# A two-block transformer kernel: masks in row tiles, a weight split on VectorE, and the last cross-attention head in halves

## The reference, cut to what matters

```python
# forgetting heads, per block of 128 queries
logits = einsum('bhqd,bhkd->bhqk', q_b, k) * scale
logits = logits + F_b[..., :, None] - F[..., None, :]
logits = where(k_pos[None, :] <= q_pos[:, None], logits, NEG_INF)
p = softmax(logits);  out = einsum('bhqk,bhkd->bhqd', p, v)
# differential heads: mask is k // 64 <= q // 64
p = softmax(masked l1) - lam * softmax(masked l2)
# cross-attention, 4 heads of 256, after both layers' mixers
q = split_heads(rms_norm(x) @ wq);  k, v = split(rms_norm(mem) @ wkv)
out = softmax(q k^T * 256**-0.5) v
```

## Time and profile before

| | |
|---|---|
| median of 3 runs | 2654.91 us (2652.19 to 2660.30) |
| profiled execution | 2654.79 us, span 2653.0 us |
| TensorE, products | busy 2494.0 us (94%) |
| TensorE, weight loads | busy 1854.0 us (70%) |
| VectorE, ScalarE, GpSimd | 1141.5, 948.8, 1001.1 us |
| mean granted TensorE clock | 0.980 |
| attention stage | 20 to 250 us |
| cross-attention, layer 0 and 1 | 297 to 440 us and 1135 to 1276 us |

### The profile page before, as it was taken

The page is one execution under the profiler, slowest core; times in us unless marked ns, Lnnn a source line. Parts: engine busy times, 40 slices in busy tenths (PEclk is TensorE's granted clock), DMA queues, the critical chain, the costliest instruction groups (busy, mean ns, idle before and its releaser), DMA issues. The chain is left out here.

```text
span 2653.0 us, 38681 instructions
## 1 busy us (share of the span) xinstructions
PE 2494.0 (94%) x15264; PEld 1854.0 (70%) x15264; DVE 1141.5 (43%) x1581; ACT 948.8 (36%) x1372; POOL 1001.1 (38%) x496
## 2 busy tenths in 40 slices
PE   8999999999999999999999999999998999599996
PEld 5776787788877788878678887777586786333334
DVE  5443422566653623342356656343754414311113
ACT  5443432444432444242344442343423213111112
POOL 5321531444457432251344437642223432223320
PEclk9999999999999999999999999999999999799998
DMA  3111331322257211232222226421001215699992
GB/s 134 72 48 40 104 111 49 103 91 92 78 205 232 85 64 48 80 112 74 85 95 95 95 87 236 169 95 71 1 4 50 80 63 181 238 395 336 361 370 105
DMA packets 76281, 333.88 MB, mean 126 GB/s; under 512 B 17113, under 2 KB 21209, under 8 KB 51801
## 3 DMA queue, kind: packets, MB, share of 16 engines
q1 hardware_dynamic: 62336, 313.98, 33.2%
q0 software_dynamic: 13824, 18.19, 2.0%
HBM read 372.67 MB, written 16.78 MB: 147 GB/s over the span
## 5 line engine op out<-in xcount | busy, mean ns | idle before, releaser
L227 PE MATMUL bank<-dense_s_hi,dense_w_hi 128*128 128x512 f32 x672 | 267.1, 397 | 12.7 <-POOL dense_w_lo L711 6.5
L228 PE MATMUL bank<-dense_s_lo,dense_w_hi 128*128 128x512 f32 x672 | 261.9, 390 | 0.0
L229 PE MATMUL bank<-dense_s_hi,dense_w_lo 128*128 128x512 f32 x672 | 261.8, 390 | 0.0
L711 POOL TENSOR_TENSOR dense_w_lo<-weights,dense_w_hi 128x1024 fp32r<-128x1024 f32 x77 | 200.1, 2598 | 93.7 <-ACT dense_w_hi L680 90.3
L1517 DVE TENSOR_TENSOR hidden<-up_y 128x512 f32 x44 | 158.2, 3595 | 64.6 <-ACT up_y L1481 64.0
L229 PE MATMUL bank<-xn_r,weights_r 128*128 128x512 f32 x448 | 176.0, 393 | 0.0
L1978 DVE SCALAR_TENSOR_TENSOR xn<-mix,xn 128x1024 f32<-128x1024 f32 x64 | 114.0, 1782 | 116.0 <-DMA mix<-in_modulation 105.0
L227 PEld LDWEIGHTS bank<-dense_s_hi,dense_w_hi 128*128 128x128 f32 x672 | 126.0, 188 | 53.5 <-POOL dense_w_lo L711 14.7
L1494 POOL TENSOR_TENSOR up_w_lo<-weights,up_w_hi 128x2048 fp32r<-128x2048 f32 x22 | 101.6, 4616 | 126.8 <-ACT up_w_hi L1469 126.8
L229 PEld LDWEIGHTS bank<-dense_s_hi,dense_w_lo 128*128 128x128 f32 x672 | 126.2, 188 | 26.8
L227 PE MATMUL bank<-xn_r,mix_r 128*128 128x512 f32 x352 | 140.8, 400 | 2.8 <-POOL up_xn_lo_r L359 2.5
(11 more groups left out here) (743 smaller groups left out, 6247.6 us busy)
## 6 DMA issues: line engine op xcount, KB each, us to landing
weights<-in_w_up SPq DMA_DIRECT2D x44, 1024.0 KB, 4.9
mix<-in_modulation SPq DMA_DIRECT2D x64, 512.0 KB, 5.1
weights<-in_w_xattn SPq DMA_DIRECT2D x24, 1024.0 KB, 4.9
weights<-in_experts_up SPq DMA_DIRECT2D x24, 1024.0 KB, 12.3
moe_weights<-in_experts_up SPq DMA_DIRECT2D x24, 1024.0 KB, 14.6
weights<-in_w_down SPq DMA_DIRECT2D x44, 512.0 KB, 3.8
rec_rkv<-in_experts_up SPq DMA_DIRECT2D x16, 1024.0 KB, 10.5
weights<-in_w_attn SPq DMA_DIRECT2D x8, 1536.0 KB, 6.4
```

The lines of the kernel that those rows point to most:

```text
L227: nc.tensor.matmul(out, left.hi, right.hi, start=first, stop=False)
L228: nc.tensor.matmul(out, left.hi, right.lo, start=False, stop=False)
L229: return nc.tensor.matmul(out, left.lo, right.hi, start=False, stop=last)
L711: nc.gpsimd.tensor_tensor(w[b].lo[:, :], units.rows(b, 0, D, 0, D), w[b].hi[:, :], ALU.subtract).then_inc(w_split, 1)
```

## The change

In the attention stage:
- The masks are added by row-tiled products as the query-key products are: m = 0 on partitions 0 to 63, m = 1 on 64 to 127. For a differential unit one pair of 64-row products is enough, for a forgetting unit there are two pairs. ScalarE builds the five matrices for it with 15 copies instead of 3, behind the gate's exponential and ahead of the rounding of unit 1's weights.
- The middle third of unit 0's weights is split by VectorE and no longer by GpSimd; it stands behind the norm and ahead of the gate's column z. The selector `pick` is made behind the logs.
- The second transposes of the last unit go to banks 7, 3, 4 and 5 and no longer wait for the copies out of banks 6, 0, 1 and 2.

In the cross-attention:
- At the start, four idle products stand ahead of the keys, the table of the square root is loaded ahead of the squares and no longer first of all, each mean stands behind a key product of the second half, and the queries' weights are rounded behind all squares and ahead of the root.
- In the last head, the second half of the values product of head 2 stands behind the logits, with four idle products behind it; VectorE normalises in two halves, the transposes follow by halves, the two copies run on ScalarE and VectorE, the values product goes to banks 4 and 5 and over the memory rows first, and the last copy out is made by VectorE.

```diff
-                        for bank, m, places in (one, two):
-                            mm = nc.tensor.matmul(g.bank[bank][:, c + keys - P:c + keys], eye_r[:, :],
-                                                  (causal_r if u in FOX_UNITS else chunked_r)[:, :], start=False, stop=True)
-                            if n == len(places) - 1:
-                                mm.then_inc(logits_done, 1)
+                        masks = ((eye_r[0], causal_r[0]), (eye_r[1], causal_r[1])) if u in FOX_UNITS else ((eye_r[0], chunked_r),)
+                        for left, right in masks:
+                            for bank, m, places in (one, two):
+                                half = slice(m * HALF, (m + 1) * HALF)
+                                mm = nc.tensor.matmul(g.bank[bank][:, c + keys - P:c + keys], left[half, :], right[half, :],
+                                                      start=False, stop=left is masks[-1][0])
+                                if n == len(places) - 1 and left is masks[-1][0]:
+                                    mm.then_inc(logits_done, 1)
...
-                for turned in (turned_even, turned_odd):
-                    pe.wait_ge(turned, (groups[u] + 4 * m) // 2)
+                if turned_into(u, m) is TURNED:
+                    for turned in (turned_even, turned_odd):
+                        pe.wait_ge(turned, (groups[u] + 4 * m) // 2)
...
-            for t, t_r in ((g.ident, eye_r), (g.causal, causal_r), (g.chunked, chunked_r)):
-                mask = nc.scalar.activation(t_r[:, :], t[:, :], ACT.Copy)
-            mask.then_inc(masks_ready, 1)
             read_queries(0)
             act.wait_ge(gate_abs, 1)
             nc.scalar.activation(gate_e, gate_e, ACT.Exp, scale=-1.0).then_inc(gate_exp, 1)
+            for to, rows, columns, source, at in (
+                    (eye_r[0], low, both, g.ident, both), (eye_r[0], high, left, g.ident, right), (eye_r[0], high, right, g.ident, left),
...
+                nc.scalar.activation(to[rows, columns], source[rows, at], ACT.Copy).then_inc(masks_ready, 1)
             round_weights(1)
...
             norm.gpsimd(pool)
-            for j in range(1, 3):
-                first_rest(j)
+            first_rest(2)
...
             norm.vector(dve)
+            dve.wait_ge(w_rounded, 2)
+            nc.vector.tensor_tensor(first_part(w[0].lo, 1), first_part(whole[0], 1), first_part(w[0].hi, 1), ALU.subtract)\
+              .then_inc(middle_split, 1)
...
+                        if m == 1 and k == KT - 1:
+                            mm.then_inc(proj_done, 1)
+                        if first and m == 1:
+                            norm.tensor_mean(pe, k)
...
+            def last_step(i):
+                logits(i)
+                mix_values(i - 1, 1)
+                idle_products(g, 2, 4)
+                pe.wait_ge(mixed, 2 * i + 1)
+                for b in range(2):
+                    pe.wait_ge(last_p, b + 1)
+                    for t in range(2):
+                        for qb in (2 * b, 2 * b + 1):
+                            mm = nc.tensor.transpose(g.bank[6 + t][:, qb * P:(qb + 1) * P], probs[:, qb, t * P:(t + 1) * P], g.ident[:, :])
+                        if b == 1:
+                            mm.then_inc(turned_done, 1)
                 pe.wait_ge(v_ready, i + 1)
+                for t in range(2):
+                    pe.wait_ge((pT_ready, last_pT)[t], (2 * i + 1, 1)[t])
+                    for m in range(2):
+                        mm = nc.tensor.matmul(g.bank[4 + m][:, :], v[:, t, m * P:(m + 1) * P], probs_T[:, t, :],
                                               start=(t == 0), stop=(t == 1))
...
-            norm.tensor_means(pe)
             values(0, first=True)
...
-            norm.scalar_table(act)
...
-            norm.scalar_squares(act, lambda: round_weights(0, QUERY))
+            norm.scalar_squares(act)
+            round_weights(0, QUERY)
             norm.scalar_root(act)
...
+            def last_step(i):
+                dve.wait_ge(values_done, 2 * i)
+                read_values(i)
+                for b in range(2):
+                    here = slice(2 * b, 2 * b + 2)
+                    dve.wait_ge(exp_done, 2 * i + b + 1)
+                    nc.vector.reciprocal(inv[:, here], total[:, here]).then_inc(inv_ready, 1)
+                    dve.wait_ge(inv_ready, i + b + 1)
+                    for qb in (2 * b, 2 * b + 1):
+                        p = nc.vector.tensor_scalar(probs[:, qb, :], probs[:, qb, :], inv[:, qb:qb + 1], None, ALU.mult)
+                    p.then_inc(last_p, 1)
```

More of the change, by code:

```diff
@@ L316, in tensor_means, with tensor_mean @@
         for k in range(KT):
[L317 to L321, removed]
+            self.tensor_mean(pe, k)
+    def tensor_mean(self, pe, k):
+        g = self.g
+        pe.wait_ge(self.squared, k + 1)
+        for b in range(TT):
+            mm = g.nc.tensor.matmul(self.bank[32 * b:32 * b + 32, 0:P], g.mean_all[:, 0:32], g.square[:, k % 2, b * P:(b + 1) * P],
+                                    start=(k == 0), stop=(k == KT - 1))
+        mm.then_inc(self.summed, 1)
     def tensor_spread(self, pe):
@@ L783 @@
 TURNED = (6, 0, 1, 2)
+LAST_TURNED = (7, 3, 4, 5)
 def stage_attention(g, units, coming):
@@ L797, in stage_attention @@
     STARTS = (0, 32, 64, 96)
+    turned_into = lambda u, m: LAST_TURNED if (u, m) == (UNITS - 1, 1) else TURNED
     K = STARTS[-1] + FOX_HEADS
@@ L1084, in _ @@
             own.did(nc.vector.tensor_scalar(sub_gain[:, :], g.col("subln"), 1.0 - LAMBDA_INIT, None, ALU.mult))
-            own.wait()
-            own.did(nc.vector.tensor_scalar(pick[:, :, :], heads[:, :].unsqueeze(2).broadcast_to([K, FOX_HEADS, P]), -1.0, None, ALU.mult))
-            dve.wait_ge(gate_done, 1)
-            nc.vector.tensor_scalar(z[:, :], g.bank[6][0:FOX_HEADS, :], g.col("fox_bf", rows=FOX_HEADS), None, ALU.add).then_inc(gate_read, 1)
             zt = gate[0]
@@ L1103, in _ @@
                   .then_inc(log_ready, 1)
+            own.did(nc.vector.tensor_scalar(pick[:, :, :], heads[:, :].unsqueeze(2).broadcast_to([K, FOX_HEADS, P]), -1.0, None, ALU.mult))
             def split_sums():
@@ L1265, in queries, with logits @@
                     mm.then_inc(proj_done, 1)
-            def step(i, later):
+            def logits(i):
                 pe.wait_ge(q_ready, 2 * i + 2)
@@ L1276, in step, with mix_values @@
                     mm.then_inc(logits_done, 1)
-                if later:
-                    keys_values(i + 1)
+            def mix_values(i, m):
+                pe.wait_ge(pT_ready, 2 * i + 2)
+                pe.wait_ge(v_ready, i + 1)
+                for t in range(2):
+                    mm = nc.tensor.matmul(g.bank[6 + m][:, :], v[:, t, m * P:(m + 1) * P], probs_T[:, t, :],
+                                          start=(t == 0), stop=(t == 1))
+                mm.then_inc(values_done, 1)
+            def step(i, later):
+                if later == 0:
+                    last_step(i)
+                    return
+                logits(i)
+                keys_values(i + 1)
                 pe.wait_ge(p_ready, i + 1)
@@ L1388, in step @@
                 p.then_inc(p_ready, 1)
-                if later:
-                    rest(i + 1)
-                    read_keys(i + 1)
+                rest(i + 1)
+                read_keys(i + 1)
                 for t in range(2):
```

76 lines of the change are left out of this document (50 added, 26 removed).

## The result

The changed kernel takes 2635.69 us (median of 4 runs, 2631.44 to 2638.19), beside 2654.19 (4 runs, 2652.19 to 2660.30) for the kernel before: the ratio is 0.9933, with a 95% interval from 0.9921 to 0.9945. The medians differ by 18.5 (the ratio gives 17.8), and 19.6 was forecast. The profiled execution took 2638.19, its span is 2636.3, and the mean granted clock is 0.984 (0.980 before).

A forecast was written before the change was run, and what follows sets the result against it. TensorE, busy for nearly the whole attention stage, was taken as the bound there. Savings of 9.0 + 0.7 + 1.0 + 0 + 8.9 = 19.6 us from 2654.8 gave 2635.2; 2629 to 2643 held the forecast and rivals A, B and C.

The forecast's parts named there:

- Part 1: Attention units: masks in row tiles save TensorE switching and exposed weight loads; 9.0 us saved, bounds 5.5 and 11.
- The 0.11 for a pair behind another: Row-tiled pairs on TensorE: halves load side by side, so each pair's weight load adds about 0.11 us.
- The 0.09 for a change of tiling: TensorE around mask blocks: going from one tiling to the other costs 0.09 us, the same assumed for the way in.
- The lower bound of 5.5: Mask saving without the two switching terms: 0.37 - 0.11 a differential place, 0.37 - 0.22 a forgetting one, 32 places.
- the rule on loads: Trainium skill: weight loads overlap running products only in another row group; mask gain would then be near 5.5 us.
- Rival B: Masks gain less: loads behind running products (3.5 less) or VectorE and ScalarE set units (5.2 less); 2639 to 2640, chance 0.13.
- Part 2: Start: VectorE splits the middle third of the first weights, removing TensorE's wait on GpSimd; 0.7 us saved.
- the forecast's bound of 0.72: Upper bound on the saving from VectorE's split: TensorE's wait for the middle third; lower bound 0.
- Part 3: End of attention stage: last unit's second transposes into other banks; values product starts 1.0 us earlier, bounds 0.7 and 1.4.
- Part 4: Cross-attention entries, reordered: +0.3 and -0.3 us, counted as nothing; bounds 1.5 lost, 2 won.
- Part 5: Cross-attention last heads: 4.5 us saved in layer 0 (about 2.9 of it the clock), 4.4 in layer 1.
- Rival A: Clock still falls in the last head of one or both layers: 2637 to 2642 us, chance 0.30.

The follow-up runs named there:

- experiment 1: Changed kernel with the masks over all 128 rows again (three mask copies, not 15), rest kept: 2642.25 us, ratio to before 0.9954.
- Experiment 4: Kernel before with the row-tiled masks alone (no VectorE split, old end of the stage, old cross-attentions): 2649.36 us, ratio to before 0.9979.
- experiment 9: Changed kernel with the last unit's second transposes into the old banks: 2640.22 us in one run.
- Experiment 6: Changed kernel with the queries' weights rounded between the squares again, rest of the new entry kept: 2638.46 us in one run.
- experiments 5 and 10: 5: changed kernel, old cross-attention entry, 2633.87 us. 10: changed kernel repeated, 2637.01; with head norm behind unit 5's normalising, old entry order, idle products kept, 2633.90.
- experiment 2: Changed kernel with the old last head in both cross-attentions, new entry and attention stage kept: 2644.04 us, ratio to before 0.9964.
- experiment 3: Changed kernel without the four idle products of the last head: 2633.90 us, ratio to before 0.9928.

## Why the prediction was right, point by point

**Part 1, forecast 9.0.** Taking the masks alone out gives 8.75 of the stage. Unit by unit the forecast was 1.0, 1.5 (three times), 1.1, 0.2, 1.1 and 1.1; from one unit's logits to the next one's, 0.82, 1.53 (three times), 1.02, 0.05, 1.11 and, in the last unit, 1.15 were measured (experiment 1 against the kernel after). Unit 0 differs by 0.12 between kernels that are the same there, so its gain is 0.8 to 0.9. A differential unit's logits last 2.75 (2.8 forecast), a forgetting unit's 3.85 (3.9; 171.00 to 174.85). The 0.11 for a pair behind another is seen in the places of 128 keys: three pairs in 0.33, and five in 0.56 in a forgetting unit. The 0.09 for a change of tiling was read for one direction and taken for the other, and no run parts it from the exposed load. Their sum held over a unit and not place by place: 0.41, 0.46, 0.46 and 0.27 were saved in the four places of a differential unit, where the forecast had 0.46 for each and took 0.3 off once. The lower bound of 5.5 was added up wrong: 16 places at 0.26 and 16 at 0.15 are 6.6, and the 8.75 measured lies above that too, so by size as well as by the rows the rule on loads fails here. Unit 5 swallowed its gain for the reason given: the wait there was forecast at near 1 and is 0.82. Rival B had this in five units; in units 1 to 4 and 6 no wait for exponentials appeared.

**Part 2, forecast 0.7.** The wait of 0.72 is gone. VectorE's split ran from 34.23 to 35.70, after waiting for ScalarE's rounding, where 36.4 was forecast, and was in time. The start became 1.85 shorter, which is two things. 0.50 lies ahead of the stage (ScalarE's first copy comes at 19.68, at 20.18 before), where nothing was changed; over the kernels of the experiments this copy stands between 18.88 and 20.29, so I do not credit the change with it. The other 1.35 is inside the stage, from that copy to the transposes of column z: 19.39 before, 18.04 after. Experiment 4, which keeps GpSimd's split, takes 19.36; of the eleven kernels with VectorE's split nine take 18.03 to 18.05, and two, in which the clock stood at 0.50 for 6.8 us there and not for 3.4, take 18.30 and 18.39. So the split is worth 1.3 where the low clock is short, as in the kernel after, and 1.0 to 1.1 where it is long, as in the kernel before. Both lie above the forecast's bound of 0.72. This term was mis-sized because it was read off the idle time, and the time lost is the distance between starts. TensorE at the middle third, with GpSimd's split (experiment 4):

```profile
35.60 0.40 PE L229 MATMUL bank<-xn_r,weights_r 128*128 128x512 f32 x1
37.04 0.50 PE L227 MATMUL bank<-xn_r,attention_w_hi 128*128 128x512 f32 x1 [1.04 <-POOL weights_r L1072]
```

and with VectorE's (kernel after):

```profile
36.02 0.39 PE L229 MATMUL bank<-xn_r,weights_r 128*128 128x512 f32 x1
36.25 0.39 PE L227 MATMUL bank<-xn_r,attention_w_hi 128*128 128x512 f32 x1
```

The two starts are 1.44 apart with the wait and 0.23 without it, and the next product comes another 0.10 later. The mask copies took 3.2 (3.0 forecast).

**Part 3, forecast 1.0.** 1.20 by experiment 9, inside its bounds. TensorE's next wait is VectorE's copy (0.71), as foreseen.

**Part 4, forecast +0.3 and -0.3.** This term was mis-sized too: -0.27 and -0.61. The root was forecast well: in layer 0 it came 14.48 behind the start of its stage, 0.43 earlier than the 14.91 before (0.5 forecast), and in layer 1 at 13.35 against 13.42. What follows the root was charged too little: 20.23 and 20.22 instead of 19.54, so 0.69 more in each layer. GpSimd's late half holds VectorE's subtraction (0.69 more, 0.4 counted), and it holds GpSimd's own tiles of the normalised input too, which I did not count: TensorE waits for these twice, 0.7 in all, where it waited once, 0.3, before. Experiment 6 shows this part: the second wait is gone and the distance is 19.54 again, while the root comes 0.51 and 0.22 later, so that 0.18 and 0.46 come back.

The clock hid a second loss. In layer 1 the new entry ran at 1.00 throughout, and the one before had the clock at 0.50 for 3.4 us. The old entry at 1.00 has its root at 13.02 and 12.97 (experiments 5 and 10) and takes 32.56 and 32.53, so the new one is 1.0 longer: 0.69 behind the root and some 0.35 ahead of it. These 0.35 belong to the means between the key products and the moved table load, which no run takes apart; a product with its mean took 0.91 (their starts in layer 0), where 0.8 was forecast. In layer 0 the old entry was never seen wholly at 1.00. It took 34.90 with the clock at 0.50 for 6.8 us, and 34.44, 33.89 and 33.72 with 3.4 us of it; the new one took 34.7, always at 1.00.

**Part 5, forecast 4.5 and 4.4.** 4.47 and 4.39. From the logits of the last head to the end of the last copy 13.2 was forecast (421.5 to 434.7) and 13.27 measured (409.84 to 423.11), to the start of the products 8.9 and 8.87. Rival A, the clock falling again, did not come about in any kernel with the new order, with or without the idle products; experiment 2 shows that with the old order it falls in both layers, which costs 3.1 of 4.7 (2.9 of 4.5 forecast).

**The sum.** 19.9 by parts against 19.6: the terms were off by +1.1 (start), +0.1 (stage), -0.6 and -0.3 (entries) and 0 (last heads), and these mostly cancel. Of the +1.1, 0.5 stands ahead of the changed part and 0.6 is the split. The total landed within 0.5 us of the forecast partly by luck, since untouched stretches alone move one execution by several us.

## What to carry to other kernels

Where small full-row products stand between row-tiled ones, cost the switch and the exposed weight load from the start-to-start distances of the timeline; putting the small product into the same tiling can be worth more than the distance that the timeline shows behind it (0.37): a place of 128 keys fell from 0.79 to 0.33. Size a wait by the distance between the starts around it and not by the idle time alone. After shortening a bound engine, look for the one unit in which another engine has extra work, since that unit gives nothing until this work is moved. And close a long gap ahead of a block of products with work that has to be done anyway: half a values product went in here, and the filler behind it was superfluous.

## What the runs showed of the hardware that was not expected

- With almost the same bursts and the same waits (1.24 and 0.56) at the end of the attention stage, the clock fell to 0.50 for 6.8 us in the kernel of experiment 4 and stayed at 1.00 in those of before and of experiment 9, in the one trace of each. It cost 2.7 of a stage gain of 9. Why it fell in the one and not in the others stays open.
- TensorE idle for 1.60 and 0.66 around a burst of 1.29 did not lower the clock (experiment 3); 3.23 and 0.94 around one of 1.09 did, in both layers (experiment 2).
- Three row-tiled pairs of 128 columns started within 0.33 and five within 0.56, though each of their weight loads lasts 0.19: the loads ran beside products on the same row halves.
- TensorE's stall at the middle third cost more than its idle time: 1.3 for an idle of 1.04 (experiment 4 against the kernel after).
- Stretches that no edit touches differ by up to 4.6 us (694.9 to 699.5) and 7.5 us (1375.2 to 1382.7) between kernels.
